# Expert routing by a slot-to-token table, rows gathered per expert, and down weights read in pairs of rows

## The chip, the cores and the metric

The kernel runs on one core of a Trainium2 chip. The core has a matrix engine (TensorE, PE in the rows, with its weight loads as PEld), a vector engine (VectorE, DVE), a scalar engine (ScalarE, ACT), a general engine (GpSimd, POOL) and a queue engine that mostly issues transfers (SyncE, SP); sixteen DMA engines move data between the chip's memory and the on-chip buffer. The metric is device time of one execution in microseconds (us); less is better.

## The reference, cut to what matters

The program is one decoder step of two layers over 512 prompt tokens and 32 sample tokens, 544 rows of 1024 floats. Each layer has a mixer (a delta rule in the first, latent attention in the second) and then a hierarchical mixture of experts. The change touches the mixture only:

```
def hier_moe(x, w_rg, b_rg, w_re, b_re, w_gate, w_up, w_down):
    t = x.reshape(-1, shp[-1])                                   # 544 x 1024, normed
    p_group = softmax(t @ w_rg + b_rg)                           # 4 groups
    g_val, g_idx = lax.top_k(p_group, 1)
    e_logit = (t @ w_re + b_re).reshape(T, N_GROUPS, EXP_PER_GROUP)   # 4 x 8
    e_in = take_along_axis(e_logit, g_idx ...)[:, 0]
    e_val, e_idx = lax.top_k(e_in, TOP_K)                        # 2 of the 8
    gate = g_val * softmax(e_val)
    expert_id = g_idx * EXP_PER_GROUP + e_idx
    ...
    h = silu(t @ wg) * (t @ wu)          # per expert: 1024 -> 256
    y += (h * cw[:, None]) @ wd          # 256 -> 1024
```

Everything is float32. One expert has 3 MB of weights (gate, up and down, 1 MB each), 32 experts make 96 MB a layer.

## The kernel before, in words

The work is a row of blocks; at the end of a block all engines wait for one another. `experts(l, ...)` (L1482) runs once per layer. Its parts, in order:

- The output projection of the mixer (L1427 and after), while SP loads the weights of experts 2 to 4.
- `norm_transposed` (L277): the 544 rows in five chunks (four of 128, one of 32) are normed into `scaled_rows`, turned by PE into `uT`, and multiplied with the router weights as each chunk is ready (`chunk_logits`, L1552; the sums stand in `pp[2]`). SP loads the weights of experts 0 and 1.
- The routing block (L1568 to L1701). DVE makes group and expert choices as one-hot tables of 128 rows x (5 chunks x 32 experts) in a chain of small instructions, each of which waits for the one before. PE counts, with a triangle of ones, how many earlier rows chose the same expert (the rank, L1677 to L1679). DVE turns rank and expert into a row number in a list sorted by expert, and POOL scatters all normed rows, twice (first and second choice), to `sorted_rows` in the chip's memory: ten indirect DMAs (L1695). DVE meanwhile makes the tables that are needed only later: gates, overflow tables, and the place of each row's result. The block ends when all of it has ended.
- The main expert block (L1818 to L1897). Each expert has 64 slots. SP fetches, five experts ahead (`DEEP`): gate and up weights (L1530, L1531) as soon as PE is done with the ones five before, the 64 rows that stand at the expert's base in the sorted list (`fetch_rows`, L1725; the base is read from a table into a register), and the down weights (L1534). PE's order for expert e (`step`, L1840) is: half of gate and up (L1757), turning the hidden tile of e-1 (L1767), turning the rows of e+1 (`turn`, L1745, which waits for those rows), the other half of gate and up, down of e-1 (L1777). DVE copies the turned rows with the norm's gains (`keep_tile`, L1784), multiplies gate and up (`hidden`, L1790) and copies the turned hidden tile (`keep_hidden`, L1795). ACT does silu (L1801), copies the result from PSUM and stores it (L1808, L1811) to `expert_rows`.
- The overflow block (L1900), whose loop runs once for each 64 rows beyond an expert's first 64. The trace has no matmul between the two expert parts and the combining part, in neither layer: no expert has more than 64 rows here.
- The combining block: POOL gathers the result rows of every token (L1968, five chunks x two choices), DVE adds them with their gates (L1978).

Of the kernel before, what the change touches and what calls it, by code (L numbers as in the profile page):

```python
# [8 lines left out]
P = 128  # L9
# [7 lines left out]
D = 1024  # L17
# [20 lines left out]
XS_ROWS = 2 * T + SLOTS  # L38
# [6 lines left out]
def shape_constants():  # L45
# [27 lines left out]
    parts["over_shift"] = SLOTS * (np.arange(P)[:, None] + 1)  # L73
# [36 lines left out]
def build(nc, I, O, debug=()):  # L110
    ctx = ExitStack()
    with ctx:
# [164 lines left out]
        def norm_transposed(tag, src, rows, gain_to, sync_extra=None, kept_rows=None, on_chunk=None, sums=None):  # L277

            n = len(rows)
            with ExitStack() as cx:  # L280
                norm = Norm(tag, src, rows, gain_to, cx, kept_rows, sums)
                with nc.Block() as block:
# [3 lines left out]
                    @block.scalar  # L286
                    def _(act):
                        norm.act_part(act)

# [22 lines left out]
        xs = nc.dram_tensor("sorted_rows", (XS_ROWS, D), F32, kind="Internal").ap()  # L312
        ys = nc.dram_tensor("expert_rows", ((NE + OVER) * SLOTS, D), F32, kind="Internal").ap()
        over_rows = nc.dram_tensor("over_table", (P, 2), I32, kind="Internal").ap()
# [176 lines left out]
        zero = sb("zero_rows", [SLOTS, D // 2], where=IN)  # L491
# [3 lines left out]
        with nc.Block() as block:  # L495
# [4 lines left out]
            def _(sp):  # L500
# [3 lines left out]
                sp.dma_start(xs[2 * T:XS_ROWS, :].rearrange("s (q d) -> s q d", q=2), bc(zero[:], 1, 2)).then_inc(s_st, 16)  # L504
                for q in range(2):
                    sp.dma_start(ys[NE * SLOTS:, q * 512:(q + 1) * 512].rearrange("(j s) d -> s j d", s=SLOTS), bc(zero[:], 1, OVER)).then_inc(s_st, 16)
# [6 lines left out]
                sp.wait_ge(s_st, 80)  # L513
# [968 lines left out]
        def experts(l, halves, prefetch=None):  # L1482
# [4 lines left out]
            with ME:  # L1487
# [18 lines left out]
                base_i = mb("base_int", [P, NE], I32)  # L1506
                over_i = mb("over_int", [P, 2], I32)
# [3 lines left out]
                dw = I["w_exp_down"][l].rearrange("e (j p) n -> e p j n", p=P)  # L1511

                class Lane:
# [3 lines left out]
                    def __init__(self, tag, deep, two, outs):  # L1517
                        self.deep, self.two, self.outs = deep, two, outs
# [7 lines left out]
                main = Lane(f"moe{l}", DEEP, 2, DEEP)  # L1526
                over = Lane(f"over{l}", 1, 1, 1)
# [5 lines left out]
                def fetch_down(sp, s, k, expert):  # L1533
                    sp.dma_start(slots[k][:, 4096:6144].rearrange("p (j n) -> p j n", j=2), dw[expert]).then_inc(s.wd[k], 16)  # L1534
# [24 lines left out]

                s_lg = sem(f"route{l}_logits")  # L1560
                norm_transposed(f"normf{l}", x, ROWS, [(G_FFN + l, uT)], kept_rows=xn, sync_extra=weights_in_ring, on_chunk=chunk_logits, sums=x_sums)
                RT = ExitStack()
                with RT:
                    w1, w2, oh1, oh2, em, rank, before, sc, ge, tb, ov, real = in_uT(
                        *[[P, NCH, NE]] * 6, [P, NCH + 1, NE], [P, 12, NCH], [P, NCH, NG], [P, 9, NE], [P, 2], [P, 1])
                    s_d, s_a, s_r, s_z, s_sc = (sem(f"route{l}_{m}") for m in ("dve", "act", "ranks", "table", "scattered"))
                    steps = {}
                    with nc.Block() as block:  # L1568
                        @block.vector
                        def _(dve):  # L1570
                            d = Chain(dve, s_d)
                            gb4 = small[:, 12 + 36 * l:48 + 36 * l]
                            d(V.memset(before[:, 0, :], 0.0))
                            d(V.tensor_scalar(real[:], const("rows"), float(NS), None, ALU.is_lt))
                            d(V.memset(lg[:], 0.0))
                            dve.wait_ge(s_lg, NCH)
                            own = slice(l * (NG + NE), (l + 1) * (NG + NE))
                            d(V.tensor_tensor(lg[:, 0:NC_P, :], pp[2][:, 0:P * NC_P].rearrange("p (c n) -> p c n", n=P)[:, :, own],
                                              bc(gb4, 1, NC_P), ALU.add))
                            d(V.tensor_tensor(lg[0:NS, NC_P, :], pp[2][0:NS, P * NC_P:P * NC_P + NR3][:, own], gb4[0:NS, :], ALU.add))  # L1580
                            gl, el = lg[:, :, 0:NG], lg[:, :, NG:]
                            gmax, gval, v1, v2, m1, t, r1, a1, o1, lt = (sc[:, k, :] for k in range(10))

                            d(V.tensor_reduce(gmax, gl, AX, ALU.max))
                            d(V.tensor_tensor(ge[:], gl, bc(gmax, 2, NG), ALU.subtract))
                            steps["group"] = d.n
                            dve.wait_ge(s_a, 1)
                            d(V.tensor_reduce(gval, ge[:], AX, ALU.add))
                            d(V.reciprocal(gval, gval))
                            first = const("first_of_4")  # L1590
                            d(V.tensor_tensor(ge[:], gl, bc(gmax, 2, NG), ALU.is_equal))
                            d(V.tensor_tensor(ge[:], ge[:], bc(first, 1, NCH), ALU.mult))
                            d(V.tensor_reduce(t, ge[:], AX, ALU.max))
                            d(V.tensor_tensor(ge[:], ge[:], bc(t, 2, NG), ALU.is_equal))

                            g8 = ge[:].rearrange("p c g -> p (c g)")
                            fl = lambda a: a.rearrange("p c (g e) -> p (c g) e", e=EPG)
                            w1g = w1[:].rearrange("p c (g e) -> p (c g) e", e=EPG)
# [4 lines left out]
                            for k, (v, oh) in enumerate(((v1, oh1), (v2, oh2))):  # L1603
                                d(V.tensor_reduce(v, em[:], AX, ALU.max))
                                d(V.tensor_tensor(oh[:], em[:], bc(v, 2, NE), ALU.is_equal))
                                d(V.tensor_tensor(oh[:], oh[:], bc(const("first_of_32"), 1, NCH), ALU.mult))
                                d(V.tensor_reduce(m1, oh[:], AX, ALU.max))
                                d(V.tensor_tensor(oh[:], oh[:], bc(m1, 2, NE), ALU.is_equal))
                                if k == 0:
                                    d(V.scalar_tensor_tensor(em[:], oh[:], -BIG, em[:], ALU.mult, ALU.add))  # L1610
                            d(V.tensor_tensor(w1[:], oh1[:], oh2[:], ALU.add))
                            d(V.tensor_scalar(w1[:, NC_P, :], w1[:, NC_P, :], real[:], None, ALU.mult))
                            for c in range(NCH):
                                d(V.tensor_tensor(before[:, c + 1, :], before[:, c, :], w1[:, c, :], ALU.add))
                            d(V.tensor_tensor(t, v2, v1, ALU.subtract))
                            steps["chosen"] = d.n
                            dve.wait_ge(s_a, 2)
                            g1, g2 = gate[:, 0, :], gate[:, 1, :]
                            d(V.tensor_scalar(g1, t, 1.0, None, ALU.add))
                            d(V.reciprocal(g1, g1))  # L1620
                            d(V.tensor_tensor(g1, g1, gval, ALU.mult))
                            d(V.tensor_tensor(g2, g1, t, ALU.mult))

                            dve.wait_ge(s_r, 1)
                            d(V.tensor_copy(rank[:], pp[0][:, 0:NE * NCH].rearrange("p (c n) -> p c n", n=NE)))
                            cnt, base, no, oin, ob, A, Bt, sel, tmp = (tb[:, k, :] for k in range(9))
                            d(V.tensor_copy(cnt, pp[1][:, 0:NE]))
                            one = ones[:, 0:NE]
# [1074 lines left out]
```

## Time and profile before

| what | us |
|---|---|
| median of three runs (from 1968.8 to 1972.33) | 1970.95 |
| profiled execution, its own time | 1965.26 |
| span of the profiled execution | 1963.1 |
| PE busy | 1556.3 (79%) |
| DVE busy | 625.8 (32%) |
| ACT busy | 374.7 (19%) |
| POOL busy | 120.9 (6%) |

The span is the part of the execution that the trace covers; 2.16 us lie around it. Busy time of PE is the time of its matmuls, whatever clock they ran at. In the trace the first layer's routing block begins near 714 us and its experts end near 1065; the second layer's begin near 1576 and end near 1920.

### The profile page before, as it was taken

To read this page: it belongs to the slowest core of one execution; us is meant where nothing else is said; L and a number is where in the kernel's file an instruction comes from. 1 tells how busy PE (TensorE), PEld (TensorE's weight loads), DVE (VectorE), ACT (ScalarE), POOL (GpSimd) and SP (SyncE) were. 2 spreads that over 40 slices of the span, in tenths; PEclk is the share of its full clock that TensorE was granted. 3 is DMA by queue.
4 is the path that set the end of the run, shared out by engine and by line. 5 is a ranking of instruction groups with operands and counts; after the bars stand their busy time and mean duration, and the time that the engine had idled before them with its cause. 6 is when DMAs were issued, how large, how long until landed. Compare 5 with 4: busy or idle time off the path is not lost. (4 is left out here: it accounts for less than half of the span.)

```text
span 1963.1 us, 23745 instructions
## 1 busy us (share of the span) xinstructions
PE 1556.3 (79%) x9093; PEld 1063.8 (54%) x9093; DVE 625.8 (32%) x1399; ACT 374.7 (19%) x975; POOL 120.9 (6%) x114
## 2 busy tenths in 40 slices
PE   6999987998768946777775499999879829777771
PEld 3788565998656434444443366666565515444440
DVE  3455116564351052111111533555430252111114
ACT  2243104443031010100000112224230101000001
POOL 0000012011400010000001000001000010000002
PEclk9999986999657977978788699999888969887886
DMA  9611000001431447999995500305154249999974
GB/s 304 140 65 65 28 1 1 1 1 43 149 118 49 189 169 260 355 342 352 335 341 179 188 15 21 156 1 201 69 172 193 97 150 343 343 350 361 363 271 163
DMA packets 109723, 340.83 MB, mean 174 GB/s; under 512 B 16327, under 2 KB 44591, under 8 KB 91663
## 3 DMA queue, kind: packets, MB, share of 16 engines
q1 hardware_dynamic: 92098, 284.04, 42.2%
q0 software_dynamic: 7296, 38.80, 5.4%
q10 hardware_dynamic: 10240, 16.79, 2.5%
q8 instruction: 58, 0.95, 0.2%
q14 instruction: 31, 0.25, 0.0%
HBM read 301.42 MB, written 38.17 MB: 173 GB/s over the span
## 5 line engine op out<-in xcount | busy, mean ns | idle before, releaser
L1757 PE MATMUL pp<-ring,uT 128*64 128x256 f32 x2048 | 304.7, 451 | 1.6 <-DVE uT L1784 1.6
L1757 PEld LDWEIGHTS pp<-ring,uT 128*64 128x64 f32 x2048 | 163.6, 160 | 123.7 <-issue 75.0
L1745 PE MATMUL pp<-consts,scaled_rows 64*128 64x64 f32 x512 | 70.0, 291 | 167.5 <-DMA scaled_rows<-sorted_rows 167.5
L1745 PEld LDWEIGHTS pp<-consts,scaled_rows 64*128 64x128 f32 x512 | 61.3, 201 | 178.1 <-issue 176.6
L1777 PE MATMUL pp<-ring,uT 128*64 128x512 f32 x512 | 137.9, 664 | 1.1 <-ACT uT L1808 1.1
L541 PE MATMUL pp<-uT,ring 128*128 128x272 f32 x576 | 135.2, 393 | 0.9 <-PEq L342 0.9
L541 PEld LDWEIGHTS pp<-uT,ring 128*128 128x128 f32 x576 | 108.0, 190 | 22.2 <-issue 1.0
L1445 PE MATMUL pp<-ring,uT 128*128 128x512 f32 x256 | 115.7, 615 | 4.0 <-PEq L126 4.0
L1801 ACT ACTIVATE uT<-pp 128x128 f32<-128x128 f32 x64 | 17.8, 278 | 464.0 <-PE pp L1757 464.0
L1784 DVE TENSOR_TENSOR uT<-pp,gains 128x512 f32<-128x512 f32 x64 | 44.3, 692 | 194.7 <-PE pp L1745 194.7
L1445 PEld LDWEIGHTS pp<-ring,uT 128*128 128x128 f32 x256 | 50.5, 198 | 67.7 <-issue 67.7
L1795 DVE COPY uT<-pp 128x128 f32<-128x128 f32 x64 | 18.7, 292 | 205.3 <-PE pp L1767 205.3
L1777 PEld LDWEIGHTS pp<-ring,uT 128*64 128x64 f32 x512 | 44.3, 166 | 65.4 <-issue 60.4
L1790 DVE TENSOR_TENSOR uT<-uT,pp 128x128 f32<-128x128 f32 x64 | 18.4, 288 | 153.9 <-ACT uT L1801 153.9
L1968 POOL DMA_INDIRECT ring<-expert_rows,row_index x20 | 22.7, 1135 | 660.8 <-PEq L1951 655.3
L1808 ACT ACTIVATE uT<-pp 128x512 f32<-128x512 f32 x64 | 38.2, 597 | 108.7 <-PE pp L1777 108.7
L1468 DVE TENSOR_TENSOR x<-x,pp 128x512 f32<-128x512 f32 x16 | 11.0, 687 | 105.9 <-PE pp L1445 105.9
L274 PE MATMUL pp<-consts,norm_xn 128*128 128x128 f32 (+1 forms) x80 | 13.2, 325 | 39.2 <-DVE norm_xn L258 39.2
L1695 POOL DMA_INDIRECT sorted_rows<-scaled_rows,row_index x20 | 19.2, 959 | 403.9 <-DVE row_index L1636 398.4
L561 PE MATMUL pp<-ring,uT 128*128 128x512 f32 (+1 forms) x128 | 43.5, 503 | 0.0
L1458 ACT ACTIVATE scaled_rows<-x 128x1024 f32<-128x1024 f32 (+1 forms) x10 | 10.6, 1056 | 144.2 <-DVE x L1468 137.2
L2434 PE MATMUL pp<-consts,ring 128*128 128x128 f32 (+1 forms) x288 | 35.2, 275 | 0.8 <-PEq L2272 0.8
(580 smaller groups left out, 2451.9 us busy)
## 6 DMA issues: line engine op xcount, KB each, us to landing
ring<-in_w_exp_gate SPq DMA_DIRECT2D x64, 1024.0 KB, 22.3
ring<-in_w_exp_up SPq DMA_DIRECT2D x64, 1024.0 KB, 26.7
ring<-in_w_exp_down SPq DMA_DIRECT2D x64, 1024.0 KB, 26.9
scaled_rows<-sorted_rows SPq DMA_DIRECT2D x64, 256.0 KB, 25.9
expert_rows<-uT ACTq DMA_DIRECT2D x128, 128.0 KB, 7.4
ring<-in_w_in_a SPq DMA_DIRECT2D x4, 3072.0 KB, 12.2
expert_rows<-zero_rows SPq DMA_DIRECT2D x2, 2176.0 KB
x<-in_x_prompt SPq DMA_DIRECT2D x2, 2048.0 KB, 11.1
```

The costliest lines, as they stand in the source:

```text
L541: TE.matmul(pp[n % 2][:, at], w[:, j, ct * P:(ct + 1) * P], uT[:, j, t], start=(j == 0), stop=(j == DJ - 1))
L561: ins = TE.matmul(pp[c % 2][:r, o:o + k], uT[:, j, offset(c):offset(c) + r], w[:, j, o:o + k], start=(j == 0), stop=(j == DJ - 1))
L1445: ins = TE.matmul(pp[n // 2][:, (n % 2) * 512:(n % 2) * 512 + 512], mergedT[:, j, offset(c):offset(c) + P], w[:, j, :], start=(j == 0), st ...
L1695: pool.indirect_dma_start(xs, bass.IndirectOffsetOnAxis(idx[:r, c, k:k + 1], 0), xn[:r, c, :], None).then_inc(s_sc, 16)
L1745: ins = TE.transpose(pp[3][:, j * SLOTS:(j + 1) * SLOTS], xv[:, j, :], ident[:SLOTS, :SLOTS])
L1757: ins = TE.matmul(pp[0][q * SLOTS:(q + 1) * SLOTS, b * 512:b * 512 + 2 * P], xT[b][:, j, :], w[:, :, j, q * P:(q + 1) * P], start=(j == 0) ...
L1777: ins = TE.matmul(pp[2][q * SLOTS:(q + 1) * SLOTS, 0:512], hT[b][:, j, :], w[:, j, q * 512:(q + 1) * 512], start=(j == 0), stop=(j == 1))
L1784: V.tensor_tensor(xT[b][:], pp[3][:, 0:DJ * SLOTS].rearrange("p (j t) -> p j t", j=DJ), bc(gains[:, G_FFN + l, :], 2, SLOTS), ALU.mult).th ...
L1795: V.tensor_copy(hT[b][:], pp[1][:, 0:2 * SLOTS].rearrange("p (j t) -> p j t", j=2)).then_inc(s.hT, 1)
L1808: act.activation(yr[b][:], pp[2][:, 0:512], ACT.Copy).then_inc(s.y, 1)
L1968: pool.indirect_dma_start(parts[n][:r, :], None, ys, bass.IndirectOffsetOnAxis(idx[:r, c, 2 + k:3 + k], 0)).then_inc(s_y[n], 16)
L2434: ins = TE.transpose(key_bank[n % NKB][0:m, t * P:(t + 1) * P], src[t], ident)
```

## The change

Every normed chunk is stored, unsorted, to `normed_rows` by ACT's queue while the norm runs. The routing block is gone as a block: its first part (`choose`, on DVE, and `rank_tokens`, on PE) stands at the start of the main expert block. From the ranks DVE makes, per choice and chunk, a one-hot table of slots, and PE multiplies it with a table of token numbers, so that a 64 x 32 table in PSUM holds, for each slot of each expert, the number of its token. One DVE copy makes it integer (`token_of_slot`). POOL then gathers each expert's 64 rows by its column of that table, one indirect DMA for each expert. The later tables are made by DVE between experts: gates after expert 6, overflow counts after 8, overflow experts after 10, places after 12 and 14. DVE's loop over experts is written out. SP no longer loads rows or bases.

The down weights are read as pairs of neighbouring rows of `w_exp_down` (partition p holds rows 2p and 2p+1, 8 KB in one piece), and to fit, PE's gate and up matmuls take every second column of their weights (`q`). The zero stores at the program's start are cut into four of 256 columns instead of two of 512, and the one to `sorted_rows` is gone. The overflow loop loads its rows one at a time.

```
+            norm.act_part(act)
+            if rows_out is not None:
+                for c, r in enumerate(rows):
+                    act.wait_ge(norm.scaled, c + 1)
+                    act.dma_start(rows_out[offset(c):offset(c) + r, :], norm.xn[:r, c, :]).then_inc(rows_stored, 16)
...
-   zero = sb("zero_rows", [SLOTS, D // 2], where=IN)
+   zero = sb("zero_rows", [SLOTS, D // 4], where=IN)
...
-   dw = I["w_exp_down"][l].rearrange("e (j p) n -> e p j n", p=P)
+   dw = I["w_exp_down"][l].rearrange("e (p j) n -> e p (j n)", p=P)
...
    choose, on DVE (what differs from the chain of before)
+   d(V.memset(em, -BIG))
...
-   d(V.tensor_copy(w1g, bc(g8, 2, EPG)))
-   d(V.tensor_tensor(em[:], el, w1[:], ALU.mult))
-   d(V.tensor_scalar(w1[:], w1[:], -1.0, BIG, ALU.add, ALU.mult))
-   d(V.tensor_tensor(em[:], em[:], w1[:], ALU.add))
+   d(V.copy_predicated(by_group(em), bc(ge.bitcast(U32), 3, EPG), by_group(el)))
...
-   for c in range(NCH):
-       d(V.tensor_tensor(before[:, c + 1, :], before[:, c, :], w1[:, c, :], ALU.add))
...
+   dve.wait_ge(s_r, 1)
+   for k, (oh, r, hot) in enumerate(((oh1, r1, hot1), (oh2, r2, hot2))):
+       d(V.tensor_tensor(w2, oh, pp[0][:, 0:NE * NCH].rearrange("p (c n) -> p c n", n=NE), ALU.mult))
+       d(V.tensor_reduce(r, w2, AX, ALU.add))
+       d(V.tensor_tensor(hot, bc(const("slots"), 1, NCH), bc(r, 2, SLOTS), ALU.is_equal))
+       steps[f"slots{k}"] = d.n
...
+   dve.wait_ge(s_r, 2)
+   V.tensor_copy(tok_i[:], pp[3][0:SLOTS, 0:NE]).then_inc(s_t, 1)
...
    rank_tokens, on PE
+   TE.matmul(pp[0][:, 0:NE * NCH], const("upper"), w1..., start=True, stop=False)
+   for c in range(NC_P):
+       ins = TE.matmul(pp[0][:, NE * (c + 1):NE * NCH]..., ones, bc(w1[:, c, :], 1, NC_P - c), ...)
+   for c in range(NCH):
+       ins = TE.matmul(pp[1][:, 0:NE], ones, w1[:, c, :], start=(c == 0), stop=(c == NCH - 1))
+   for k, (hot, on) in enumerate(((hot1, on1), (hot2, on2))):
+       pe.wait_ge(s_d, steps[f"slots{k}"])
+       for c in range(NCH):
+           ins = TE.matmul(pp[3][0:SLOTS, 0:NE], hot[:, c, :], on[:, c, :], ...)
...
-   w = slots[k % s.deep][:, 0:4096].rearrange("p (g j n) -> p g j n", g=2, j=DJ)
+   w = slots[k % s.deep][:, 0:4096].rearrange("p (g j n q) -> p g j q n", g=2, j=DJ, q=2)
...
    the main block
+   @block.gpsimd
+   def _(pool):
+       pool.wait_ge(s_xs, 16 * NCH)
+       pool.wait_ge(s_t, 1)
+       for e in range(NE):
+           pool.wait_ge(main.turned, e + 1)
+           pool.indirect_dma_start(xg[:, e % DEEP, :], None, xs, bass.IndirectOffsetOnAxis(tok_i[:, e:e + 1], 0)).then_inc(main.x[e % DEEP], 16)
...
+   for e in range(1, NE):
+       step(e, e % STEP, last=e == NE - 1)
+       if e == 6:
+           make_gates(dve, d)
...
```

On POOL, the place is all that follows the first layer's mixer. The rows before, where `sorted_rows` is the list sorted by expert:

```order
L1690 UNCONDITIONAL_BRANCH
L1695 DMA sorted_rows<-scaled_rows,row_index 1152x1024 x10
L1568 UNCONDITIONAL_BRANCH
L1963 UNCONDITIONAL_BRANCH
L1968 DMA ring_0<-expert_rows,row_index 128x1024 x8
L1968 DMA ring_0<-expert_rows,row_index 32x1024 x2
```

And now:

```order
L1849 UNCONDITIONAL_BRANCH
L1855 DMA scaled_rows<-normed_rows,token_of_slot 64x1024 x32
L1807 UNCONDITIONAL_BRANCH
L1999 UNCONDITIONAL_BRANCH
L2004 DMA ring_0<-expert_rows,row_index 128x1024 x8
L2004 DMA ring_0<-expert_rows,row_index 32x1024 x2
```

Ten scatters ahead of the expert block have become 32 gathers inside it, one for each expert.

On PE, the place is between the last router matmuls (into `pp`, the PSUM banks) and the first expert's gate and up. Before:

```order
L1556 MATMUL pp<-router_weights,uT 32x108 x8
L282 UNCONDITIONAL_BRANCH
L1673 UNCONDITIONAL_BRANCH
L1677 MATMUL pp<-uT,consts 128x160
L1678 MATMUL pp<-uT,consts 128x160
L1679 MATMUL pp<-uT,consts 128x32
L1568 UNCONDITIONAL_BRANCH
L1838 UNCONDITIONAL_BRANCH
L1745 MATMUL pp<-consts,scaled_rows 128x64 x8
L1757 MATMUL pp<-ring,uT 64x256 x8
```

And now:

```order
L1564 MATMUL pp<-router_weights,uT 32x108 x8
L284 UNCONDITIONAL_BRANCH
L1860 UNCONDITIONAL_BRANCH
L1632 MATMUL pp<-uT,consts 128x160
L1634 MATMUL pp<-uT,consts 128x128
L1634 MATMUL pp<-uT,consts 128x96
L1634 MATMUL pp<-uT,consts 128x64
L1634 MATMUL pp<-uT,consts 128x32
L1637 MATMUL pp<-uT,consts 128x32 x5
L1642 MATMUL pp<-uT 64x32 x10
L1734 MATMUL pp<-consts,scaled_rows 128x64 x8
L1746 MATMUL pp<-ring,uT 64x256 x8
```

Three matmuls have become twenty, and one block boundary (the branch at L1568) is gone between them and the first turn (L1745, now L1734).

On SP, the place is one expert's fetch inside the loop. Before:

```order
L1822 TENSOR_LOAD base_int
L1822 ISA x2
L1732 REGISTER_ALU
L1530 ISA
L1530 DMA ring<-in_w_exp_gate 128x2048
L1531 DMA ring<-in_w_exp_up 128x2048
L1728 ISA
L1728 DMA scaled_rows<-sorted_rows 64x1024
L1534 DMA ring<-in_w_exp_down 128x2x1024
```

And now:

```order
L1722 REGISTER_ALU
L1538 ISA
L1538 DMA ring<-in_w_exp_gate 128x2048
L1539 DMA ring<-in_w_exp_up 128x2048
L1542 DMA ring<-in_w_exp_down 128x2048
```

The row load between up and down has left SP's queue, and the down weights have one piece per partition.

## Rows read from the trace of the kernel before

**Rows 1.** Page, costliest groups: busy, mean ns | idle before, releaser

```profile
L1745 PE MATMUL pp<-consts,scaled_rows 64*128 64x64 f32 x512 | 70.0, 291 | 167.5 <-DMA scaled_rows<-sorted_rows 167.5
L1795 DVE COPY uT<-pp 128x128 f32<-128x128 f32 x64 | 18.7, 292 | 205.3 <-PE pp L1767 205.3
```

**Rows 2.** Busy time by stretch: zero stores, weight loads alone, expert loop

```profile
core 0: us, PE busy (x) PEld busy (x) DVE busy (x) ACT busy (x) POOL busy (x), PEclk, DMA share, GB/s
57.00:81.00 24.00, 24.00 (x112) 19.31 (x111) 12.09 (x29) 5.59 (x18) 0.00 (x0) 1.00 0.97 198
...
800.00:1050.00 250.00, 190.37 (x1129) 103.84 (x1125) 29.23 (x69) 20.02 (x47) 0.00 (x0) 0.82 1.01 340
...
646.50:650.00 3.50, 3.50 (x10) 1.59 (x9) 0.69 (x1) 0.00 (x0) 0.00 (x0) 1.00 1.01 419
828.50:832.00 3.50, 1.91 (x17) 0.97 (x13) 0.29 (x1) 0.57 (x1) 0.00 (x0) 1.00 1.01 241
832.50:838.50 6.00, 4.47 (x24) 2.90 (x26) 0.69 (x1) 0.00 (x0) 0.00 (x0) 0.54 1.03 412
839.00:842.50 3.50, 3.50 (x24) 1.50 (x20) 0.29 (x1) 0.67 (x2) 0.00 (x0) 0.88 0.98 226
```

**Rows 3.** Timeline, layer 0, routing: start, us, instruction, [idle before <- releaser]

```profile
714.19 0.09 DVE L1573 MEMSET uT<- 128x32 f32 x1 [3.46 <-PEq L282]
...
715.58 0.18 DVE L1585 TENSOR_TENSOR uT<-logits,uT 128x20 f32<-128x20 f32 x1
...
716.55 0.18 DVE L1591 TENSOR_TENSOR uT<-logits,uT 128x20 f32<-128x20 f32 x1
...
717.40 0.24 DVE L1599 COPY uT<-uT 128x160 f32<-128x160 f32 x1
...
718.67 0.32 DVE L1604 TENSOR_REDUCE uT<-uT 128x5 f32<-128x160 f32 x1
...
723.24 1.09 DVE L1614 TENSOR_TENSOR uT<-uT 128x32 f32<-128x32 f32 x5
...
724.59 0.90 PE L1677 MATMUL pp<-uT,consts 128*128 128x160 f32 x2 [10.76 <-DVE uT L1615]
...
726.39 0.32 DVE L1625 COPY uT<-pp 128x160 f32<-128x160 f32 x1 [0.72 <-PE pp L1679]
...
729.00 1.18 POOL L1695 DMA_INDIRECT sorted_rows<-scaled_rows,row_index  x1 [188.71 <-DVE row_index L1636]
...
742.54 0.17 DVE L1671 CAST row_index<-uT 128x5 int32<-128x5 f32 x1
...
751.10 1.12 PE L1745 MATMUL pp<-consts,scaled_rows 64*128 64x64 f32 x8 [24.82 <-DMA scaled_rows<-sorted_rows]
```

**Rows 4.** Timeline, layer 1: first turn of rows

```profile
1613.34 1.12 PE L1745 MATMUL pp<-consts,scaled_rows 64*128 64x64 f32 x8 [25.39 <-DMA scaled_rows<-sorted_rows]
```

**Rows 5.** Timeline: router matmuls ahead of the routing block

```profile
700.82 3.12 PE L1556 MATMUL pp<-router_weights,uT 128*128 128x108 f32 x16
```

**Rows 6.** Timeline, combining block: a gather and its first user

```profile
1071.71 0.98 POOL L1968 DMA_INDIRECT ring<-expert_rows,row_index  x1 [330.19 <-PEq L1951]
...
1076.19 1.28 DVE L1978 SCALAR_TENSOR_TENSOR x<-ring,gates,x 128x1024 f32<-128x1024 f32 x1 [5.09 <-DMA ring<-expert_rows,row_index]
```

**Rows 7.** Timeline, expert 30's rows, layer 0 and layer 1

```profile
1042.78 1.11 PE L1745 MATMUL pp<-consts,scaled_rows 64*128 64x64 f32 x8 [4.15 <-DMA scaled_rows<-sorted_rows]
...
1899.53 1.11 PE L1745 MATMUL pp<-consts,scaled_rows 64*128 64x64 f32 x8 [4.08 <-DMA scaled_rows<-sorted_rows]
```

**Rows 8.** Timeline, two neighbouring experts at full clock, weights there

```profile
766.17 1.90 PE L1757 MATMUL pp<-ring,uT 128*64 128x256 f32 x16
...
772.77 1.90 PE L1757 MATMUL pp<-ring,uT 128*64 128x256 f32 x16
```

**Rows 9.** Timeline, weight loads of columns 32 bytes apart and of neighbouring ones

```profile
706.34 0.97 PEld L274 LDWEIGHTS pp<-consts,scaled_rows 128*128 128x128 f32 x8
707.23 1.87 PEld L1556 LDWEIGHTS pp<-router_weights,uT 128*128 128x128 f32 x16
```

More of the change, by code:

```diff
@@ L275, in turn, with norm_transposed @@
                 ins.then_inc(self.turned, 1)
-        def norm_transposed(tag, src, rows, gain_to, sync_extra=None, kept_rows=None, on_chunk=None, sums=None):
+        def norm_transposed(tag, src, rows, gain_to, sync_extra=None, kept_rows=None, on_chunk=None, sums=None, rows_out=None, rows_stored=None):
             n = len(rows)
@@ new lines, in experts @@
+                ge2 = kept[:, 988:1008].rearrange("p (a b) -> p a b", a=NCH)
+                w1, em, on1, on2, hot1, hot2, ge, real = in_uT(*[[P, NCH, NE]] * 4, *[[P, NCH, SLOTS]] * 2, [P, NCH, NG], [P, 1])
+                s_d, s_a, s_r, s_t, s_z, s_ot = (sem(f"route{l}_{m}") for m in ("dve", "act", "ranks", "tokens", "table", "over_tokens"))
+                gl, el = lg[:, :, 0:NG], lg[:, :, NG:]
+                gmax, gval, v1, v2, m1, t, r1, r2, a1, lt, p1, p2 = (sc[:, k, :] for k in range(12))
@@ new lines, in count_over @@
+                def count_over(d):
+                    one = ones[:, 0:NE]
+                    d(V.tensor_scalar(no, cnt, float(SLOTS), None, ALU.is_gt))
+                    for k in range(2, -(-T // SLOTS)):
+                        d(V.scalar_tensor_tensor(no, cnt, float(SLOTS * k), no, ALU.is_gt, ALU.add))
+                    d(V.tensor_tensor_scan(oin, one, no, 0.0, ALU.mult, ALU.add))
+                    d(V.tensor_tensor(ob, oin, no, ALU.subtract))
+                    d(V.tensor_copy(n_i[:], oin[:, NE - 1:NE]))
@@ L1860, in _ @@
                         down(pe, main, NE - 1, (NE - 1) % STEP, (NE - 1) // DEEP)
-                    @block.vector
-                    def _(dve):
-                        def step(e, k, last=False):
-                            keep_hidden(dve, main, e - 1, (k - 1) % STEP)
-                            if not last:
-                                keep_tile(dve, main, e + 1, (k + 1) % STEP)
-                            hidden(dve, main, e, k)
-                        credits(None, dve, None, main)
-                        keep_tile(dve, main, 0, 0)
-                        keep_tile(dve, main, 1, 1)
-                        hidden(dve, main, 0, 0)
-                        with dve.Fori(0, loops) as i:
-                            for k in range(1, 1 + STEP):
-                                step(i * STEP + k, k % STEP)
-                        for e in rest:
-                            step(e, e % STEP, last=e == NE - 1)
-                        keep_hidden(dve, main, NE - 1, (NE - 1) % STEP)
                     @block.scalar
@@ L1917, in _ @@
                         with pe.If(n > 0):
+                            pe.wait_ge(s_ot, 1)
+                            for k in range(2):
+                                hot, tile = over_hot(k)
+                                for c in range(NCH):
+                                    ins = TE.matmul(pp[1][0:OVER, 0:SLOTS], tile[:, c, 0:OVER], hot[:, c, :], start=(k == 0 and c == 0), stop=(k == 1 and c == NCH - 1))
+                            ins.then_inc(s_ot, 1)
                             with pe.Fori(0, n) as j:
```

324 lines of the change are left out of this document (164 added, 160 removed).

## The prediction, made before the changed kernel was run

> **What bounds the kernel now.** I began with the page's costliest groups and looked for matmuls that wait. PE idles 167.5 us ahead of the turns at L1745, every bit of it put down to rows from `sorted_rows` [rows 1]: by far the largest sum that one line of the mixture waits. Then the busy time by stretch. In the loop over experts (800 to 1050) the DMA engines are busy all the time (share 1.01) while PE has work for 190.37 of 250 us [rows 2]: that stretch is bound by transfers, and PE's wait for rows is where the queue's lateness shows, not a cost that goes by itself. But the transfers don't run evenly. One expert takes 10.5 us (828.5 to 839.0, where the pattern begins again), and in 3.5 us of it only 241 GB/s move, 226 in the next, against 412 between them, with the engines as busy [rows 2]. The slow part is where the 64 rows come. Last the timeline at the loop's start: from the routing block's first instruction (714.19) to the first turn of rows (751.10) go 36.9 us, 24.82 of them PE's wait for rows [rows 3]; in layer 1 that wait is 25.39, .6 more [rows 4], so I take 37.5 there. In this stretch hardly anything that the result needs is moved except the rows themselves: it is a chain of DVE, PE, POOL, a scatter and a load. So three places count, in both layers: the start (a chain), the loop (transfers), the end (PE held by rows).
>
> **The start, step by step.** Up to the choice DVE needs 714.19 to 724.59, 10.40 us [rows 3]. Gone are the first memset (.12 with its gap), the subtraction, the wait for ACT's exp and the group sum (715.58 to 716.55, .97), the mask in four instructions (717.40 to 718.67, 1.27) and the five running sums with the difference of the two maxima (723.24 to 724.57, 1.33): 3.69. New are a memset and a predicated copy over 160 columns; the copy of 160 took .24, a reduction of 160 .32 [rows 3], so with gaps .60 for both. Leaves 7.3.
> PE's ranks: 10 matmuls, each two records as in these rows, so 20. At the low clock a record of 108 columns took 3.12/16 = .195 [rows 5], and before 160 columns took .45 [rows 3]. 20 x .195 = 3.9 and .5 for starting and the hand-over: 4.4. All narrow ones at half the price would make 2.8, all a little dearer 6.1.
> DVE then makes slot tables: per choice a product and a reduction of 160 columns out of PSUM (.36 each, by .32 of the copy at 726.39 [rows 3]) and a comparison of 320 columns (.52, an estimate from the same row by size): 1.24, twice 2.5. PE's ten small matmuls run beside the second half; five are left, 10 records x .195 = 2.0. The cast: .25.
> POOL's first gather: .3 of hand-over and, from the gather of the combining block to its first user, 1071.71 to 1076.19 = 4.48 [rows 6]; those were 128 rows, these 64. Together 4.8.
> Sum 7.3 + 4.4 + 2.5 + 2.0 + .25 + 4.8 = 21.2 instead of 36.9 and 37.5: 15.7 and 16.3, **32 us** for both layers. Block boundary and scatters are in the 36.9 and not in the 21.2. Bounds from the prices above: 20 to 38.
>
> **The end.** When expert 30's rows come, PE has waited 4.15 us in layer 0 and 4.08 in layer 1 [rows 7]. From there PE works against weights that stood ahead of these rows in SP's queue, so they are there; a gather issued five experts ahead no longer holds it: 4 us a layer, **8**. If the last weights come only then, nothing: 0 to 8.
>
> **The loop: the down weights.** A stretch with gate and up alone (8 KB pieces) moved 419 GB/s, the loop's quick stretches, with down's 4 KB pieces among them, 412 [rows 2]. At 419 the 3.15 MB of an expert take .13 us less; only a third of the bytes change, but the small pieces may be all of the difference. Twenty-four refilled experts (27 less the last ones) in two layers: 0 to 6, I take **3**.
>
> **The loop: the rows.** Today's loss per expert is 3.5 x (1 - 233/412) = 1.52 us, with 233 the mean of 241 and 226 [rows 2]. The trace has no gathers of 64 rows beside weight loads, so this is bounded. No loss at all: 256 KB as fast as weights. Middle: a 64-partition transfer has a row, the zero stores, 198 GB/s with the engines 97% busy [rows 2]; 256 KB at 198 instead of 412 take 1.32 instead of .64 us, a loss of .69 if nothing else is slowed. Top: 1.52 as now. Gathered rows come from another queue, piece by piece between weights, so that less of the stream should stand behind them; but the same 64 partitions are written. I take 1.0, between the middle and the top: .52 x 24 x 2 = **25 us**. Below nothing too: a gather that is slower than the plain load would cost what .3 more per expert makes, 14.
>
> On this place the Trainium skill has two rules that speak against the change. "SBUF — State Buffer", section "Door 1: The DMA port swizzle": a transfer's rate goes with how many of 16 ports its partitions reach, and partitions 0 to 63 reach eight; the 198 GB/s of the zero stores agree. "DMA: Bandwidth & Descriptors", section "Issuing engines are not separate DMA queues": starting transfers from another engine saves that engine's issue time and no more. By both, the loss stays between .69 and 1.52; the second alone gives 1.52, which is the first rival below.
>
> **What I cost at nothing, and its cover.** The stores of normed rows, 2.2 MB or 5.4 us at 412 GB/s a layer, run while the norm and the chain of the start (21 us) go on; they also push the ring's weights back, which are first needed by gate and up of expert 0. If they stood ahead of these, up to 5 us a layer would come back. DVE's later tables: before, all that lies between 726.39 and 742.71 is 16.3 us [rows 3], now cut in five pieces of some 3 us, each where DVE idles 205.3/64 = 3.2 us before L1795 alone [rows 1]; uncovered, 3 us each, but only as far as PE waits there and not for weights. What queues behind a table is `keep_hidden` of the same expert, and PE's down behind that. POOL's 32 gathers at about 1 us each [rows 6] wait for the turn five experts before and lead by four experts. The four zero stores move as many bytes in smaller pieces, long before the next user of SP's queue in that stage. The overflow loop, dearer now, isn't entered.
>
> **Sum.** 32 + 8 + 3 + 25 = 68. The profiled execution took 1965.26; 1897.3 after. The median lies 5.7 above the profiled execution, so **1903**. After the change PE is next: two neighbouring experts with their weights there stand 6.60 us apart (766.17, 772.77) [rows 8], well under 10.
>
> **Rivals.**
> Rows cost the same from whichever queue (same 64 partitions, same engines): 32 + 8 + 3 = 43, **1928**. For it: 198 GB/s of any 64-partition transfer, and that the engines are shared. Against it: the loss now is over twice what these bytes explain, so something of it hangs on the order.
> Rows cost nothing, because they fill gaps: 32 + 8 + 3 + 73 = 116, **1855**. Against it: the engines have no gaps (1.01), and 198.
> Slower: gate and up now read every second column of their weights, 8 bytes apart, and if PE took the moving operand at half its pace, each expert would need 2 x 1.90 = 3.8 more, 10.4 us [rows 8], and the loop would be bound by PE. From turn 0 to turn 30 that is 30 x 10.4 = 312 instead of 1042.78 - 751.10 = 291.7; less 16 of the start, +4.6 a layer, +9: **1980**. It decides from the point where an expert on PE takes more than the transfers' 10. Against it: weight loads of columns 32 bytes apart took .121 each, of neighbouring ones .117 [rows 9], so strides were free for the other operand; the moving one isn't shown.
> The same page on the SBUF names 16-byte lines that must be hit twice to be read at full pace; a stride of 8 bytes hits them twice, and so would be free. The stride of 32 bytes hits each once and shows no loss for weight loads either.
> That the change doesn't do what it says: the row loads would have to stay; the order of the queues shows them gone.
>
> **Chances and range.** Forecast (something of the rows' loss goes) .48; rows as now .32; rows free .11; PE-bound and slower .06; the rest (tables or stores uncovered) .03. The range 1858 to 1940 leaves out the rows for free, and the slower end; inside it are both main cases and the bounds of the start. A change under .2%, 4 us, can't be told from none. Faster: all but the slower case and part of the rest, .91; same .02; slower .07.
>
> **What would show it.** Start: the first turn some 21 us after DVE's first routing instruction, not 37, in both layers. Loop: 9.9 us per expert; 10.4 speaks for the first rival, 9.0 for the second; the slow stretches' GB/s tell which. Strides: gate and up's half at full clock 1.90 (free) or 3.8. End: no wait of 4 us for rows of expert 30. Wrong would be: gathers that land later than PE wants them (PE waiting for `normed_rows` throughout the loop), DVE's tables showing as PE's wait for the hidden tile after experts 6 to 14, or a first turn later than 24 us.

## The result, and the profile after

| | us |
|---|---|
| before, median of 4 runs | 1969.88 |
| changed, median of 4 runs | 1868.01 |
| ratio, 95% interval | 0.9481 (0.9442 to 0.9519) |
| predicted | 1903 (1858 to 1940) |

The kernel is faster, by 102 us where 68 were forecast. The profiled execution has a span of 1867.9 against 1963.1, so 95.2 are to be found in the traces; the rest is how the profiled executions stand to their medians. In the table of experiments below, one execution of e4_before_paired (1990.63 us) and one of e7_pool_plain (2588.67 us) were slow and are left out of the medians.

The start, in layer 0 of the changed kernel (timeline: start, length, instruction, and in brackets the idle time ahead of it and what ended it):

```profile
713.78 0.15 DVE L1585 TENSOR_SCALAR uT<-consts 128x1 f32<-128x1 f32 x1 [3.70 <-PEq L284]
...
716.19 0.34 DVE L1600 COPY_PREDICATED uT<-uT,logits 128x160 f32<-128x160 uint32 x1
...
721.16 0.90 PE L1632 MATMUL pp<-uT,consts 128*128 128x160 f32 x2 [7.98 <-DVE uT L1610]
721.85 1.75 PE L1634 MATMUL pp<-uT,consts 128*128 128x128 f32 x8
...
723.42 2.32 PE L1637 MATMUL pp<-uT,consts 128*128 128x32 f32 x10
725.85 0.32 DVE L1620 TENSOR_TENSOR route_kept<-route_kept,pp 128x160 f32<-128x160 f32 x1 [3.62 <-PE pp L1637]
...
729.72 0.18 DVE L1627 CAST token_of_slot<-pp 64x32 int32<-64x32 f32 x1 [0.85 <-PE pp L1642]
730.80 1.10 POOL L1855 DMA_INDIRECT scaled_rows<-normed_rows,token_of_slot  x1 [191.06 <-DVE token_of_slot L1627]
...
735.01 1.11 PE L1734 MATMUL pp<-consts,scaled_rows 64*128 64x64 f32 x8 [5.39 <-DMA scaled_rows<-normed_rows,token_of_slot]
```

Read the left column as a ledger: choice 713.78 to 721.16 (7.4), ranks to 725.85 (4.7), slot tables, token table and cast to 730.80 (5.0), gather to 735.01 (4.2). Together 21.23 instead of the 36.91 of [rows 3]. Layer 1 of the same trace:

```profile
1526.52 0.15 DVE L1585 TENSOR_SCALAR uT<-consts 128x1 f32<-128x1 f32 x1 [3.70 <-PEq L284]
...
1547.35 1.11 PE L1734 MATMUL pp<-consts,scaled_rows 64*128 64x64 f32 x8 [5.00 <-DMA scaled_rows<-normed_rows,token_of_slot]
```

That is 20.83. Before, the routing there began at 1575.85:

```profile
1575.85 0.09 DVE L1573 MEMSET uT<- 128x32 f32 x1 [3.46 <-PEq L282]
```

From there to the turn of [rows 4] went 37.49. The start gives 15.68 + 16.66 = 32.3 us.

The loop. First the page of the changed kernel (busy, mean ns | idle before, releaser):

```profile
L1746 PE MATMUL pp<-ring,uT 128*64 128x256 f32 x2048 | 288.5, 427 | 75.7 <-issue 46.2
...
L1784 DVE COPY uT<-pp 128x128 f32<-128x128 f32 x64 | 18.7, 292 | 275.0 <-PE pp L1756 275.0
...
L1734 PE MATMUL pp<-consts,scaled_rows 64*128 64x64 f32 x512 | 70.3, 283 | 10.4 <-DMA scaled_rows<-normed_rows,token_of_slot 10.4
```

PE's wait for rows was 167.5 us [rows 1] and is 10.4, which are the two first gathers. It now stands ahead of gate and up (L1746) instead, 75.7 us: 46.2 of them are "issue", idle time for which the profile names nothing, and 27.7 are put down to the weights of `in_w_exp_up`. Then the pace, from the turn of expert 10's rows to that of expert 30's. Before, the first of them is this row, the other stands in [rows 7]:

```profile
823.76 1.07 PE L1745 MATMUL pp<-consts,scaled_rows 64*128 64x64 f32 x8 [1.37 <-DMA scaled_rows<-sorted_rows]
```

Changed:

```profile
799.52 1.09 PE L1734 MATMUL pp<-consts,scaled_rows 64*128 64x64 f32 x8
...
986.94 1.09 PE L1734 MATMUL pp<-consts,scaled_rows 64*128 64x64 f32 x8
```

So (1042.78 - 823.76)/20 = 10.95 us per expert before, and 187.42/20 = 9.37 now; in layer 1, in the same way, (1899.53 - 1684.61)/20 = 10.75 and (1801.58 - 1612.74)/20 = 9.44. Ahead of expert 30's first half PE waits for weights, and for 1.02 us only:

```profile
992.73 2.03 PE L1746 MATMUL pp<-ring,uT 128*64 128x256 f32 x16 [1.02 <-DMA ring<-in_w_exp_up]
```

The loop's end is the last copy out of PSUM by ACT. Before:

```profile
1064.96 0.60 ACT L1808 ACTIVATE uT<-pp 128x512 f32<-128x512 f32 x1 [2.12 <-PE pp L1777]
```

Changed, with POOL's first gather of the combining block behind it:

```profile
1009.57 0.60 ACT L1797 ACTIVATE uT<-pp 128x512 f32<-128x512 f32 x1 [2.12 <-PE pp L1766]
...
1018.11 0.95 POOL L2004 DMA_INDIRECT ring<-expert_rows,row_index  x1 [63.77 <-PEq L1987]
```

From first turn to last copy 313.86 became 274.56; in layer 1 308.19 became 276.85. The loops give 39.3 + 31.3 = 70.6 us, where 36 were forecast (rows 25, end 8, pairing 3). What is given back: between that last copy and POOL's gather 6.75 became 8.54 (1071.71 in [rows 6]), in layer 1 6.36 became 8.62; combining in layer 0 and layer 1's mixer are 1.9 and 2.4 longer. 32.3 + 70.6 - 8.4 (4.1 at the two boundaries, 4.3 in combining and mixer), and .5 in the rest, make the 95.2 but for rounding. Why the boundaries cost 2 us more each was not looked into.

### The profile page after: what moved, and what is told of

It is laid out like the page before. It is cut to its first block and busy times, and to the rows that moved or that the text cites. A ratio compares the mean times of both kernels' runs of the same rounds, so it can differ in the third digit from the quotient of the medians.

```text
span 1867.9 us, 23357 instructions
## 1 busy us (share of the span) xinstructions
PE 1540.5 (82%) x9161; PEld 1057.2 (57%) x9161; DVE 618.0 (33%) x1365; ACT 374.1 (20%) x975; POOL 158.9 (9%) x158
## 5 line engine op out<-in xcount | busy, mean ns | idle before, releaser
L1746 PE MATMUL pp<-ring,uT 128*64 128x256 f32 x2048 | 288.5, 427 | 75.7 <-issue 46.2
L1746 PEld LDWEIGHTS pp<-ring,uT 128*64 128x64 f32 x2048 | 152.5, 147 | 198.4 <-issue 108.2
L1855 POOL DMA_INDIRECT scaled_rows<-normed_rows,token_of_slot x64 | 57.7, 901 | 797.9 <-DVE token_of_slot L1627 403.6
L1766 PE MATMUL pp<-ring,uT 128*64 128x512 f32 x512 | 122.0, 597 | 1.1 <-ACT uT L1797 1.1
L1734 PE MATMUL pp<-consts,scaled_rows 64*128 64x64 f32 x512 | 70.3, 283 | 10.4 <-DMA scaled_rows<-normed_rows,token_of_slot 10.4
L1734 PEld LDWEIGHTS pp<-consts,scaled_rows 64*128 64x128 f32 x512 | 61.2, 200 | 20.0 <-issue 13.8
L1766 PEld LDWEIGHTS pp<-ring,uT 128*64 128x64 f32 x512 | 37.1, 139 | 51.0 <-issue 40.6
L276 PEld LDWEIGHTS pp<-consts,norm_xn 128*128 128x128 f32 (+1 forms) x80 | 11.6, 202 | 46.6 <-DVE norm_xn L260 45.4
```

Of the source, the lines that this page charges most:

```text
L276: ins = TE.transpose(pp[c % 2][:, j * P:j * P + r], xv[:, j, :], ident[:r, :r])
L1734: ins = TE.transpose(pp[3][:, j * SLOTS:(j + 1) * SLOTS], xv[:, j, :], ident[:SLOTS, :SLOTS])
L1746: ins = TE.matmul(pp[0][q * SLOTS:(q + 1) * SLOTS, b * 512:b * 512 + 2 * P], xT[b][:, j, :], w[:, :, j, q, :], start=(j == 0), stop=(j == ...
L1766: ins = TE.matmul(pp[2][q * SLOTS:(q + 1) * SLOTS, 0:512], hT[b][:, j, :], w[:, j, q * 512:(q + 1) * 512], start=(j == 0), stop=(j == 1))
L1855: pool.indirect_dma_start(xg[:, e % DEEP, :], None, xs, bass.IndirectOffsetOnAxis(tok_i[:, e:e + 1], 0)).then_inc(main.x[e % DEEP], 16)
```

## The experiments

The question was why the loop gave twice what was forecast, and whether its loss is now at an end. Times are medians; the ratio is to the kernel before on the same chip; pace is turn 10 to turn 30 in layer 0 / layer 1 as above.

| run | median | ratio (95%) | us per expert |
|---|---|---|---|
| before | 1969.88 | | 10.95 / 10.75 |
| changed | 1868.01 | .9481 (.9442 to .9519) | 9.37 / 9.44 |
| e1_down_4k | 1873.11 | .9500 (.9439 to .9561) | 9.49 / 9.53 |
| e2_rows_by_sp | 1937.80 | .9825 (.9764 to .9887) | 10.72 / 10.67 |
| e3_five_gathers | 1793.20 | .9107 (.9044 to .9169) | 7.63 / 7.69 |
| e4_before_paired | 1963.80 | .9983 (.9936 to 1.0031) | 10.85 / 10.58 |
| e5_spread_gather | 2045.57 | 1.0368 (1.0313 to 1.0423) | 11.40 / 11.34, PE-bound |
| e6_sp_spread | 2047.36 | 1.0365 (1.0318 to 1.0412) | 11.40 / 11.39, PE-bound |
| e7_pool_plain | 1865.56 | .9454 (.9398 to .9510) | 9.39 / 9.38 |
| e8_tables_first | 1876.10 | .9492 (.9443 to .9541) | 9.48 / 9.44 |
| e9_spread_turned | 1871.26 | .9489 (.9418 to .9559) | 9.43 / 9.28 |
| e10_sp_spread_turned | 1906.94 | .9670 (.9598 to .9741) | 10.21 / 10.11 |
| e11_half_rows | 1831.93 | .9317 (.9259 to .9376) | 8.62 / 8.66 |
| e12_sp_half_rows | 1838.80 | .9359 (.9300 to .9419) | 8.74 / 8.74 |

**Pairing or rows?** The changed kernel with down in two pieces:

```
+ dw = ...rearrange("e (j p) n -> e p j n", p=P)
+ w = slots[...].rearrange("p (g j n) -> p g j n", g=2, j=DJ);  ... w[:, :, j, q * P:(q + 1) * P]
```

> The changed kernel with the down weights read as before, two pieces of 4 KB per partition, and with gate and up read in whole columns again. All else as changed. Theory R (the loop's gain, 70 us over both layers, comes from the rows leaving SP's queue, and pairing is worth what the rates 419 and 412 GB/s say): 3 to 10 us slower than the changed kernel's 1868, so 1871 to 1878. Theory P (pairing of the down rows made most of it): 30 us slower or more, 1898 and above.

5 us slower by the medians, though the two kernels' single times overlap (1862.97 to 1870.00, and 1867.86 to 1875.72); the pace is .12 and .09 us per expert longer. That is theory R, and within the .13 that the prediction allowed; theory P is out. The opposite edit, pairing alone in the kernel before:

> The kernel before with the down weights in one piece of 8 KB per partition and gate and up read in every second column; nothing else of the change. Theory R: 3 to 8 us faster than before (1970), 1962 to 1967. Theory P: 30 us faster or more, 1940 and below.

No change that can be told (ratio .9983, interval across 1): the pace is .10 to .17 better, the first ten experts are .1 to .2 slower each. Pairing is not what made the gain.

**Rows back into SP's queue, and no rows.**

```
  fetch_gate_up(sp, s, k % s.deep, expert)
+ sp.wait_ge(s.turned, e + 1)
+ sp.dma_start(xg[:, k % s.deep, :], xs[bass.ds(e * 15, SLOTS), :]).then_inc(s.x[k % s.deep], 16)
  sp.wait_ge(s.dn, e + 1)
```

> The changed kernel, but each expert's 64 rows are loaded by SP between up and down, as one plain transfer of 64 neighbouring rows of the normed rows (so the rows are not the expert's own); the gathers are left out, the table is still made and waited for. Theory R: the old loss of 1.5 us per expert comes back, so 45 to 60 us slower than the changed kernel, 1913 to 1928. Theory P: within 15 of it, up to 1883.

70 us slower, more than was expected, and with that as much as the whole of the loop's gain. And without any:

```
+ if e >= DEEP:
+     continue
  pool.wait_ge(main.turned, e + 1)
  pool.indirect_dma_start(...)
```

> The changed kernel with only the first five experts' rows gathered in each layer; the later experts work on the rows that stand in the buffer, so 27 of 32 row transfers are left out. Theory R with a rest of loss (the rows still write 64 partitions and slow the weights, some .7 us per expert as estimated from 388 GB/s in the loop against 419): 25 to 40 us faster than 1868, 1828 to 1843. Rival (gathered rows now cost nothing beyond their bytes, 256 KB at 412 GB/s = .64 us): 54 x .64 = up to 34 too where transfers bind; so it is the GB/s in the loop that tells: 410 or more with no rows speaks for a rest of loss by rows, about 388 against it. Should PE bind by then, less than 15.

75 us faster: the expectation had counted either the bytes or the loss, and both go. So in the changed kernel rows still cost 75 us, of which their bytes are 54 x .64 = 34. (The pace of 7.6 is not that of the transfers: one expert's weights and results, 3.41 MB, take 8.06 us at 423 GB/s. In these twenty experts PE uses up weights that came ahead.) Busy time by stretch shows it (stretch, length; busy PE, PEld, DVE, ACT, POOL; granted clock, share of the DMA engines, GB/s), before:

```profile
860.00:940.00 80.00, 61.64 (x359) 33.32 (x357) 9.18 (x22) 6.55 (x16) 0.00 (x0) 0.81 1.02 344
```

changed:

```profile
860.00:940.00 80.00, 63.03 (x398) 33.98 (x393) 10.18 (x24) 7.59 (x17) 7.16 (x8) 0.89 1.02 382
```

rows by SP:

```profile
860.00:940.00 80.00, 62.71 (x376) 33.33 (x377) 12.26 (x34) 6.95 (x16) 0.00 (x0) 0.81 1.02 348
```

five gathers only:

```profile
860.00:940.00 80.00, 69.34 (x490) 38.69 (x488) 12.53 (x30) 8.74 (x20) 0.00 (x0) 1.00 1.02 423
```

The engines' share is 1.02 in all four: only the last column tells that they are being held up. Rows in the weights' queue 344 to 348, in another 382, none 423.

Which packets are held up, the rows' or the weights'? The DMA queues of the same 80 us tell (packets, MB, share of the 16 engines' time; q1 is SP's queue with the weights, q0 POOL's with the rows). Changed:

```profile
q1 hardware_dynamic: 3558, 25.89, 84.6%
q0 software_dynamic: 702, 2.34, 9.8%
```

Five gathers only:

```profile
q1 hardware_dynamic: 4289, 31.24, 93.1%
```

A megabyte of weights keeps an engine busy for .931 x 16 x 80 / 31.24 = 38.1 us when no rows come, and for 41.8 beside the gathers. So the rows slow the weights too.

**The other queue, or the gather?**

```
- pool.indirect_dma_start(xg[:, e % DEEP, :], None, xs, bass.IndirectOffsetOnAxis(tok_i[:, e:e + 1], 0))
+ pool.dma_start(xg[:, e % DEEP, :], xs[e * 15:e * 15 + SLOTS, :])
```

> The changed kernel with the gathers replaced by plain loads of 64 neighbouring rows into partitions 0 to 63, issued by POOL at the same places (not the expert's own rows). If it is another queue beside the weights' that saves: 1863 to 1875, as gathers. If it is how a gather's pieces are spread over the engines: 1915 to 1940, as when SP loads them.

Like the gathers (9.39 and 9.38), so it is not the gather but whose queue the loads stand in. One thing is not separated: the profile calls POOL's queue software_dynamic and SP's hardware_dynamic, and no run loads the rows from a second queue of SP's kind, such as ACT's.

**Half of the partitions?**

```
+ for h in range(2):
+     pool.indirect_dma_start(xn[64 * h:64 * h + 32, e % DEEP, :], None, xs, <column e of a 32 x 64 table, half h>)
...
+ xv = xn[0:96, k % s.deep, :].rearrange("t (p j) -> t j p", j=DJ)
+ TE.matmul(pp[3][:, j * SLOTS:(j + 1) * SLOTS], xv[:, j, :], <64 of 96 columns of ident>, start=True, stop=True)
```

> The changed kernel with each expert's 64 rows gathered into partitions 0 to 31 and 64 to 95 (two gathers of 32 rows) instead of 0 to 63; PE turns them with a matmul over 96 partitions that picks the 64. Same bytes, same queue. Theory H (the loss that rows still cause comes from their writing only partitions 0 to 63, which move at 198 GB/s): the loop goes at 410 to 420 GB/s instead of 388, 8.7 to 8.9 us per expert instead of 9.4, 25 to 40 us less, 1828 to 1843. Theory B (any transfer of rows beside weights disturbs them): the rate stays near 388 and the time at 1865 to 1875 with a little more for PE.

> As the run with the rows loaded by SP between up and down (64 neighbouring rows, not the expert's own; 1938), but into partitions 0 to 31 and 64 to 95, two loads of 32 rows. Theory H: the queue matters only through the half of the partitions; with both halves the loss is gone in SP's queue too: 1830 to 1850. Theory Q (the rows are dear because the weights stand behind them in one queue): most of the 70 us stays, 1900 to 1940.

Both inconclusive, by a fault in their design: PE became the bound. The turn that took 1.09 us took nearly four (timeline of the third; granted clock 1.00):

```profile
754.23 3.90 PE L1739 MATMUL pp<-consts,scaled_rows 96*128 96x64 f32 x16
```

Between 860 and 940 us PE was busy all the time, in both runs.

They were repeated with transposes of all 96 partitions, DVE dropping the 32 columns between.

> Gathers into partitions 0 to 31 and 64 to 95 again, but PE turns the 96 partitions with eight transposes of 96 columns (the ones between are dropped by DVE's copy), since the matmul over 96 took 3.9 us instead of 1.09 and made PE the bound. PE should take about .6 us more per expert than in the changed kernel, 7.3 at full clock, less than the transfers. Theory H (rows are dear because they write only partitions 0 to 63): 410 GB/s or more while transfers bind, 25 to 40 us less than the changed kernel, 1828 to 1843. Theory B (any rows beside weights disturb): 388 GB/s, 1865 to 1880.

> Rows by SP between up and down (64 neighbouring rows, not the expert's own) into partitions 0 to 31 and 64 to 95, turned by eight transposes of 96 columns. Theory H: as the spread gathers within 15 us, 1830 to 1855: with all partitions reached the queue no longer matters. Theory Q (weights behind the rows in one queue): 1900 to 1940, as with 64 partitions.

The turn now took 1.03 at the same granted clock of 1.00:

```profile
780.35 1.03 PE L1739 MATMUL pp<-consts,scaled_rows 96*128 96x96 f32 x8
```

Theory H falls for the gathers: 9.43 and 9.28 us per expert and no gain in the time. Spread gathers:

```profile
860.00:940.00 80.00, 61.46 (x396) 34.43 (x395) 10.67 (x32) 7.00 (x16) 13.74 (x16) 0.88 1.02 384
```

Spread rows by SP:

```profile
860.00:940.00 80.00, 63.57 (x388) 34.64 (x386) 10.67 (x32) 7.00 (x16) 0.00 (x0) 0.85 1.02 361
```

In SP's queue the spread saved 31 us, .5 us per expert, and left the rest: 1907 lies in the range of theory Q, at its lower end.

**All partitions in one transfer.** The norm writes the halves of a row apart, the table numbers half rows, PE turns 4 blocks of 128 x 128:

```
+ out, src = out.rearrange("t (h p j) -> t p h j", h=2, p=P), src.rearrange("t (p h j) -> t p h j", h=2, p=P)
...
+ V.tensor_scalar(tok_i[:], pp[3][:, 0:NE], 2.0, upper_half, ALU.mult, ALU.add)
...
+ pool.indirect_dma_start(xn[:, e % DEEP, 0:D // 2], None, xs.rearrange("t (h d) -> (t h) d", h=2), ...)
...
+ xv = xn[:, k % s.deep, 0:D // 2].rearrange("t (p j) -> t j p", p=P)
+ for j in range(4):
+     ins = TE.transpose(pp[3][:, j * P:(j + 1) * P], xv[:, j, :], ident)
```

> Each expert's 64 rows gathered as 128 half rows of 2 KB, one in every partition (the norm writes its rows with the halves apart, the table numbers half rows, PE turns four blocks of 128 x 128); same bytes, same queue, weights as in the changed kernel. Theory A (rows disturb because their pieces are laid on other partitions than the same DMA engine writes weights to; with all 128 partitions in one transfer each engine keeps to its own): 410 GB/s or more in the loop, 8.7 to 8.9 us per expert instead of 9.4, 1830 to 1845. Theory B (any rows beside weights disturb them by as much): 385 GB/s as now, 1865 to 1880.

> 128 half rows in all 128 partitions again, but as one plain load by SP between up and down (neighbouring half rows, not the expert's own). Theory A: the queue doesn't matter once every engine keeps to its partitions; within 15 us of the gathered half rows, 1830 to 1855 if that is right. Theory Q (weights behind rows in one queue wait, whatever the partitions): 1895 to 1940.

Theory A's times in both: 8.62 and 8.66 us with gathers, 8.74 in SP's own queue, where theory Q wanted 1895 or more. The run with gathers, 1832, is 36 us faster than the changed kernel. The GB/s by 2 us, between 860 and 940 us of each trace; before:

```profile
GB/s 223 242 340 412 420 293 252 287 340 413 395 278 350 285 403 411 297 325 293 397 415 309 323 334 373 399 328 349 343 395 395 297 363 367 365 371 290 359 393 334
```

changed:

```profile
GB/s 406 331 362 414 434 414 430 305 350 418 427 335 315 413 422 312 377 415 421 430 418 358 317 410 426 299 365 421 423 422 260 354 419 421 430 315 320 425 413 322
```

gathered half rows:

```profile
GB/s 434 411 426 426 422 416 424 413 414 427 426 418 412 415 427 422 418 426 430 414 414 423 420 419 418 418 426 430 408 420 416 418 424 422 419 429 426 414 414 421
```

half rows by SP:

```profile
GB/s 432 412 420 428 408 416 429 429 414 414 415 428 417 432 412 424 420 411 435 407 434 404 427 423 421 418 417 423 422 422 421 411 420 428 416 432 401 430 415 425
```

The dips are gone in either queue, with the same bytes, and with SP waiting and issuing in the order in which it lost 2 us per expert with 64 partitions. The weights' packets are as quick as without rows, 38.4 us for a megabyte (gathered half rows):

```profile
q1 hardware_dynamic: 3952, 28.80, 86.3%
q0 software_dynamic: 720, 2.36, 7.4%
```

And the pieces became half as long with the edit, 2 KB per partition instead of 4, and no run has short pieces over 64 partitions; that shorter pieces by themselves help is not borne out by the down weights, whose pieces of 4 KB instead of 8 gained nothing (e1_down_4k). All of this is on loads: each expert's results leave in two stores of 64 partitions each in all of these stretches, the even ones too.

**Are the later tables covered?**

```
  choose(dve, d)
+ make_gates(dve, d); count_over(d); over_experts(d); place(d, 0); place(d, 1)
  keep_tile(dve, main, 0, 0)
```

> The changed kernel with gates, overflow counts, overflow experts and both places made by DVE before the first expert's tile instead of between experts 6 and 14. If these tables are covered where they stand now (the cost of nothing that was predicted), they now delay the first expert: PE has turned the first rows at 21 us and waits for DVE, which ends some 11 us after the token table, about 5 us later than the rows come; 8 to 14 us slower over both layers, 1876 to 1882. If they are not covered there, no change or faster.

8 us slower by the medians; the trace is clearer. PE's first gate and up waits for DVE's first copy of rows for 5.77 us:

```profile
740.54 3.68 PE L1746 MATMUL pp<-ring,uT 128*64 128x256 f32 x16 [5.77 <-DVE uT L1773]
```

In the changed kernel it waits for .78:

```profile
736.90 3.50 PE L1746 MATMUL pp<-ring,uT 128*64 128x256 f32 x16 [0.78 <-DVE uT L1773]
```

That is 5 us a layer. Where the tables stand now they cost nothing that the trace shows: from 772 to 860 us, where DVE makes all five in layer 0, no wait of PE is put down to DVE.

## Why the prediction was right, and where it was not

*The start: right.* 21.2 forecast, 21.23 and 20.83 measured. The parts too: choice 7.3 against 7.4, ranks 4.4 against 4.7, tables and cast 4.75 against 5.0 with the hand-over, gather 4.8 against 4.2. A chain adds up from rows of the same kind, as long as every instruction in it is counted. The bounds of 20 to 38 were wider than the prices beside them: the ranks' 2.8 to 6.1 move the sum by 1.7 us a layer at most, and no other part has bounds.

*The loop's cause: right; its size: wrong.* The term that was mis-sized is "Today's loss per expert is 3.5 x (1 - 233/412) = 1.52 us". It was read from one expert of 10.5 us (828.5 to 839.0 [rows 2]), and that was a quick one: over twenty experts the pace was 10.95 and 10.75. At the 420 GB/s of the runs with half rows an expert takes 8.6 to 8.7, so the loss was 2.1 to 2.3, and 2.0 with the rows back in SP's queue (10.7 less 8.74). The GB/s by 2 us show what the one stretch hid: before, much more time lies under 400 than 3.5 us in 10.5. [rows 2] itself had it: a mean of 340 over 250 us, against 412, is a loss of 17%, or 1.8 us in 10.5. The loss that stays after the change, taken as 1.0, measured .75 to .8 (9.37 less 8.62, 9.44 less 8.66). That this is near the middle bound of .69 is luck: that bound holds "if nothing else is slowed", but by the queues' rows most of the loss, 3.15 MB x (41.8 - 38.4) / 16 = .67, is in the weights' packets, and some .2 in the rows' own. So 1.3 to 1.6 per expert were saved rather than .52. The time came out nearer to the second rival (1855) than to the forecast (1903); the stated range held it near its lower end.

*The rivals.* "Rows cost the same from whichever queue" (1928, .32) is ruled out by the rows put back into SP's queue (+70). The rule of the Trainium skill's "DMA: Bandwidth & Descriptors", section "Issuing engines are not separate DMA queues", that another issuing engine saves its sequencer's time only, doesn't hold here: plain loads from POOL instead of SP took 72 us less (1865.56 and 1937.80). "Rows cost nothing" (1855) was nearest in time and wrong in its reason: rows cost 75 us still, 41 of them beyond their bytes. "PE-bound" and slower is out: a half of gate and up at full clock took 1.98 us, not 3.8. In the run with whole columns (e1_down_4k, the second row) it was 1.90, both at a granted clock of 1.00:

```profile
756.76 1.98 PE L1746 MATMUL pp<-ring,uT 128*64 128x256 f32 x16
775.89 1.90 PE L1746 MATMUL pp<-ring,uT 128*64 128x256 f32 x16
```

The stride cost 4%, where the weight loads of [rows 9] had suggested none; in the kernel before, too, it made 1.99 of 1.90 (e4_before_paired). The 16-byte lines of the Trainium skill's "SBUF — State Buffer", section "Door 1: The DMA port swizzle", had made it free too; the measured 4% decides.

*The end: right.* PE no longer waits for expert 30's rows. By the packets' times the last weights land 11.3 us ahead of the last copy before and 6.8 now in layer 0, 11.1 and 6.8 in layer 1: 8.8 us, where 8 were forecast. Of the 70.6 that leaves 61.8 for the loop's rows and pairing, where 28 were forecast. *Pairing: small, as forecast* (3); the 5 us by the medians are not clear of the spread. *The tables' cover: right* (5 us a layer when they stand first).

*The ports.* The Trainium skill's "SBUF — State Buffer", section "Door 1: The DMA port swizzle", gives partitions 0 to 31 eight of 16 ports, partitions 0 to 63 the same eight, and all 128 partitions 16. Theory H took the two gathers of 32 partitions together. Taken one by one each reaches eight, and they lost as much as the 64 neighbours (9.43 and 9.37); the one transfer over all 128 partitions lost nothing that the rate shows. So the rule, read for each transfer by itself, fits the gathers. It doesn't give the quarter of the loss that the spread saved in SP's queue (.5 of 2.0 us), nor that the weights beside the rows are slowed as well.

*The sum* came out 34 us short, as much as the one term of the rows; the small losses at the block boundaries (4.1 us) and in combining and mixer (4.3) were not foreseen at all.

## What to carry to other kernels

A full share of the DMA engines says nothing on what they move: put GB/s beside it, and look at it over many periods of the loop, not one. Loads into half of the partitions that ran beside loads into all of them slowed these too; moving them from SP's queue to POOL's took some 60% of that away (2.0 us per expert to .75), laying the same bytes over all 128 partitions in one transfer took all of it, in either queue. Take a loop's pace from two rows twenty rounds apart, and what it loses from its mean rate against its best.

## What the runs showed of the hardware that was not expected

- 256 KB loaded into 64 partitions cost 10.7 - 8.74 = 2.0 us per expert more than into 128 when in the weights' queue, and .75 from POOL's; two transfers of 32 partitions each were no better from POOL, and .5 better in the weights' queue.
- Most of that is in the transfers beside it: a megabyte of weights kept an engine busy for 41.8 us beside gathers into 64 partitions, 38.4 beside the same bytes into 128, and 38.1 with no rows.
- With columns 32 bytes apart as the stationary operand, plain matmuls over 96 partitions took 3.90 us for 8 blocks (16 records), eight transposes over the same 96 partitions 1.03 (8 records), both at a granted clock of 1.00.
- The moving operand read at a stride of 8 bytes took 1.98 instead of 1.90 us for 16 matmul records of 256 columns.
